# Gate table of the expert stage in stages of 64 tokens instead of 32, and the first gathered rows fetched after the last stage is stored

## The reference

```python
qry = (xb @ wq).reshape(blk, PEER_HEADS, 2, PEER_DHALF)
sc = jnp.einsum('thpd,hpkd->thpk', qry, subkeys)
s1, i1 = lax.top_k(sc[:, :, 0], 16); s2, i2 = lax.top_k(sc[:, :, 1], 16)
cand = (s1[..., :, None] + s2[..., None, :]).reshape(blk, 8, 256)
sf, ci = lax.top_k(cand, 16)
eid = e1 * 128 + e2                       # the two halves of the pick
g = softmax(sf)
act = gelu(einsum('td,thkd->thk', x, u_tab[eid]))
out = einsum('thk,thkd->td', g * act, v_tab[eid])
```

## Time and profile before

| | before |
|---|---|
| median of 3 runs | 4385.43 us (4378.03 to 4401.97) |
| profiled execution: its own time | 4393.77 us |
| profiled execution: span | 4392.1 us, granted TensorE clock 0.947 |
| TensorE (PE) busy | 3913.5 us, 89% |
| VectorE (DVE) busy | 2641.3 us, 60% |
| ScalarE (ACT) busy | 1313.7 us, 30% |
| GpSimd (POOL) busy | 1015.5 us, 23% |
| DMA, whole span | 985884 packets, 846.08 MB, 193 GB/s |

### The profile page before, as it was taken

One profiled execution on the slowest core, in us unless ns is written; L12 is line 12 of the kernel. 1 busy time (PEld: TensorE's weight loads), 2 busy tenths in 40 slices (PEclk: granted clock), 3 DMA queues, 4 the chain that ended last, 5 costly groups with the idle time before them and its releaser, 6 DMA issues.

```text
span 4392.1 us, 57633 instructions
## 1 busy us (share of the span) xinstructions
PE 3913.5 (89%) x21916; PEld 2057.0 (47%) x21916; DVE 2641.3 (60%) x4720; ACT 1313.7 (30%) x1836; POOL 1015.5 (23%) x672
## 2 busy tenths in 40 slices
PE   5999787799777899899999987999999999988987
PEld 3675342266533644455555543444444444444433
DVE  4232111577545405999899846667666766676765
ACT  4233111244224212333333332223323222222223
POOL 0000000223002000000000024444444455555642
PEclk8999898899789999999999998999999999999999
DMA  5232533422363215999977799888888899999993
GB/s 197 94 114 79 166 108 131 164 96 87 107 215 103 104 58 142 240 264 305 292 224 224 216 252 249 230 231 215 226 231 232 232 244 267 256 247 247 264 238 114
DMA packets 985884, 846.08 MB, mean 193 GB/s; under 512 B 755026, under 2 KB 835242, under 8 KB 978219
## 3 DMA queue, kind: packets, MB, share of 16 engines
q1 hardware_dynamic: 921540, 568.86, 51.9%
q0 software_dynamic: 60112, 215.78, 15.4%
q10 hardware_dynamic: 4032, 58.72, 3.3%
HBM read 620.46 MB, written 186.31 MB: 184 GB/s over the span
## 4 chain that ended last, share of the span: by engine, by line
DVE 20%; PE 14%; DMA 14%; SPq 4%; issue 4%; ACT 3%; POOL 2%; DVEq 0%; ACTq 0%; POOLq 0%
PE ex_psy L2940 9%; DMA ex_gate<-gate_all 8%; PE ex_psa L2908 4%; DMA ex_u<-in_peer_u_dram 4%; DVE rt_hotg L2659 2%; DVE rt_hote L2655 2%; SPq L2351 2%; DVE ex_acc L2783 2%; DVE ex_ulo L2615 2%; POOL ex_vlo L2458 2%; SPq L2411 2%; DVE ex_acc L2763 1%; DVE ex_wa L2797 1%; DMA ex_ug<-in_peer_u_dram,ex_idxp 1%; DVE rt_sc L2667 1%
## 5 line engine op out<-in xcount | busy, mean ns | idle before, releaser
L2940 PE MATMUL ex_psy<-ex_vhi,ex_wboth 128*128 128x512 f16 x3584 | 1107.7, 388 | 127.3 <-POOL ex_vlo L2458 77.9
L2908 PE MATMUL ex_psa<-h_hi,ex_uth 128*128 128x512 f16 (+1 forms) x2048 | 726.6, 355 | 32.1 <-DMA ex_utl<-ex_ulo 24.6
L2908 PE MATMUL ex_psa<-h_lo,ex_uth 128*128 128x512 f16 (+1 forms) x2048 | 726.5, 355 | 0.0
L2908 PE MATMUL ex_psa<-h_hi,ex_utl 128*128 128x512 f16 (+1 forms) x2048 | 726.3, 355 | 0.0
L2940 PE MATMUL ex_psy<-ex_vlo,ex_wboth 128*128 128x512 f16 x1792 | 694.4, 388 | 0.0
L2458 POOL TENSOR_TENSOR ex_vlo<-ex_v,ex_vhi 128x1024 f16<-128x1024 f32 x128 | 317.8, 2483 | 1420.2 <-ACT ex_vhi L2557 1419.9
L2940 PEld LDWEIGHTS ex_psy<-ex_vhi,ex_wboth 128*128 128x128 f16 x3584 | 356.9, 100 | 584.7 <-issue 141.1
L2548 ACT ACTIVATE ex_wboth<-ex_wa 128x896 f16<-128x896 f32 x128 | 121.6, 950 | 1080.4 <-DVE ex_wa L2797 1080.4
L2763 DVE TENSOR_TENSOR ex_acc<-ex_acc,ex_psy 128x512 f32<-128x512 f32 x434 | 289.3, 680 | 113.4 <-PE ex_psy L2940 113.2
L2908 PEld LDWEIGHTS ex_psa<-h_hi,ex_uth 128*128 128x128 f16 x2048 | 201.1, 98 | 217.7 <-DMA ex_utl<-ex_ulo 27.9
L2908 PEld LDWEIGHTS ex_psa<-h_hi,ex_utl 128*128 128x128 f16 x2048 | 201.2, 98 | 190.2 <-issue 5.2
(11 more groups left out here) (389 smaller groups left out, 6353.4 us busy)
## 6 DMA issues: line engine op xcount, KB each, us to landing
ex_u<-in_peer_u_dram SPq DMA_DIRECT2D x128, 512.0 KB, 5.8
ex_v<-in_peer_v_dram SPq DMA_DIRECT2D x128, 512.0 KB, 4.1
gate_all<-rt_stage ACTq DMA_DIRECT2D x28, 2048.0 KB, 7.1
ex_gate<-gate_all SPq DMA_DIRECT2D x128, 448.0 KB
act_all<-ex_wa SPq DMA_DIRECT2D x80, 448.0 KB, 3.3
ex_wa<-act_all SPq DMA_DIRECT2D x80, 448.0 KB, 4.8
ad_w<-in_ada_w_dram SPq DMA_DIRECT2D x8, 2048.0 KB, 9.9
sh_w<-in_w_in_dram SPq DMA_DIRECT2D x10, 1024.0 KB, 8.2
```

Source lines behind the costliest of these rows:

```text
L2908: mm = nc.tensor.matmul(ps_a[:, at:at + e - a], x[s][:, k, :], h[:, k, a:e], start=(k == 0 and j == 0), stop=(k == KD - 1 and j == 2))
L2940: mm = nc.tensor.matmul(sum_bank(q, n), w, v_[:, a * 512:(a + 1) * 512], start=(j == 0), stop=(j == len(mms) - 1))
```

## The change

`RUN` goes from 32 to 64. So `gate_all` has 14 stages of 64 tokens in place of 28 of 32, `stage` has two buffers of 32 KB a partition in place of 16 KB, a stage is full after 8 groups of 8 tokens and is stored as one DMA of 4 MB, and a block's gates are 14 runs of 256 bytes per partition. The larger buffers reach into the memory of `ug`, the buffers of the gathered u rows, so POOL's first three gathers (batch 0 of u), which were issued in the routing part, now wait until the last group is copied (`evac`) and both stage buffers are stored. SP's wait before the first v load (L2404) keeps its meaning: all stages stored. Memory moves: `wa` and `st` are allocated ahead of the routing buffers, and `same` takes the place of `cand`, which is dead when `same` is written.

```diff
-RUN = 32
+RUN = 64
...
+        wa = [sb(f"wa{s}", [P, DENSE]) for s in range(2)]
+        st = sb("st", [P, 6, PT + 1])
...
-            cand = ea("cand", [P, HEADS, TOPK * TOPK])
+            with nc.sbuf_tensor("rt_cand", [P, HEADS, TOPK * TOPK], F32) as cand:
+                pass
+            same = ea("same", [P, 2, HEADS, TOPK, TOPK], F16)
...
-            wa = [sb(f"wa{s}", [P, DENSE]) for s in range(2)]
-            st = sb("st", [P, 6, PT + 1])
...
                 pool.wait_ge(picked, 7)
                 pool.wait_ge(moved, 32)
+                pool.wait_ge(evac, GROUPS_A)
+                for e in range(2):
+                    pool.wait_ge(stage_stored[e], DENSE // RUN // 2 * 16)
                 gather("peer_u", ug, u_rows, 0, dotted)
...
-                    m, q = g // 4, g % 4
+                    m, q = g // (RUN // BT), g % (RUN // BT)
...
-                    if q == 3:
+                    if q == RUN // BT - 1:
```

More of the change, by code:

```diff
@@ L2271, in experts @@
             numbers = ea("numbers", [P, 2, HEADS, TOPK, TOPK], F16)
-            same = ea("same", [P, 2, HEADS, TOPK, TOPK], F16)
             ranks = ea("ranks", [P, TOPK, TOPK], F16)
```

## The result

| | before | after |
|---|---|---|
| median | 4382.27 us (4378.03 to 4401.97, 4 runs) | 4315.36 us (4307.24 to 4317.01, 4 runs) |
| ratio | | 0.9835, 95% interval 0.9802 to 0.9868 |
| profiled execution: span, clock | 4392.1 us, 0.947 | 4314.2 us, 0.954 |

The change makes the kernel 67 us faster.

The account below looks back on a forecast made before the run. From 1890 us on TensorE had the most work, with the gate load on nearly every group's path. Terms -27 - 29 - 6 + 32 + 5 = -25 us gave 4361 us from the median 4385.4; range 4322 to 4408.

Parts of the forecast that it names:

- Part 1, the gate load: Output part: half as many runs per gate load shorten VectorE's gate waits; -27, -29 and -6 us, together -62 us.
- 1.4 us a load: Output part: saving per gate load, somewhat under the 1.8 us bound from 3.4 us at 136 GB/s against 1.6 at 287.
- 62 of 100 us of idle time: Output part, after 2702 us: of TensorE's about 100 us idle, shorter gate loads and v's earlier issue recover 62.
- SP's relief makes TensorE the bound: Rival, output part: v and u leave SP's queue at once, the idle 100 us go; 4322 us, chance 0.15.
- Part 2, the stores: Routing part: 4 MB stores hold the next block's transposes 5.3 us longer, stalling TensorE; 22 plus 10, +32 us.
- what queues behind the transposes on SP: Routing part: the store of `wa`, for which ScalarE waits, and the next u load are delayed; +10 us.
- stores cost more than the reads gain: Rival, routing part transposes: 13 stores at 6 us cost 78 us against -62 and +5; 4406 us, chance 0.15.
- Part 3, the start: Start of the output part: longer last store 5.3, late u gathers 4.0, shorter gate loads -4; +5 us (0 to +10).
- The gates are not read faster: Rival, gate load: a 256-byte run takes as long as two of 128, nothing comes back; 4422 us, chance 0.10.
- mechanism of a wide pitch: Gate load: runs 4 MB apart instead of 2 might read slower; skill's copies: 103 GB/s against 164.
- The transposes are not held by the larger store: Rival, routing part: queues taken in turn let transposes between the store's packets, so stores cost nothing; 4328 us, chance 0.10.

Follow-up runs that it names:

- experiment 1: Changed kernel, but the table in DRAM stays in 28 stages of 32 tokens, so gates are read in 128-byte runs: 4435.33 us, ratio 1.0112 to the kernel before.
- experiment 2: Changed kernel with each block's gates read as two DMAs of 128-byte runs from the table of 64-token stages: 4443.8 us, ratio 1.0165 to the kernel before.
- experiment 3: Changed kernel with the first 7 stages of gates read in 256-byte runs, the last 7 as two DMAs of 128-byte runs: 4411.72 us, ratio 1.0072.
- experiment 4: Changed kernel with the gate load issued as three DMAs, all in 256-byte runs: 4353.26 us, ratio 0.9935 to the kernel before.
- Experiment 5: Kernel before with the gate loads issued from ScalarE's queue instead of SP's, still in 128-byte runs: 4353.12 us, ratio 0.9926.
- experiment 7: Changed kernel with each stage stored in four DMAs of 1 MB, one after every second group: 4269.25 us, ratio 0.9752 to the kernel before.
- experiment 8: Changed kernel with each stage stored as four DMAs of 1 MB, all issued together when it is full: 4307.45 us, ratio 0.9823 to the kernel before.
- experiment 9: Changed kernel with the store of `wa` issued ahead of the transposes on SP in the routing part: 4291.58 us, ratio 0.978 to the kernel before.
- Experiment 10: Kernel before with only POOL's new wait, holding the first three gathers of u rows: 4385.13 us, ratio 0.997.

## Why the prediction was off, by its own steps

**Part 1, the gate load: the step that failed.** The mechanism was right (experiments 1 to 4): fewer runs, shorter landing, less waiting at the group's end. The size was wrong in two terms.

- *1.4 us a load.* In the kept groups the landings in the chain shrank by 2.5 us (14.98 to 12.5), and VectorE's gate waits by 46 us where I had 27; in groups 21 on by 81 where I had 29. My price came from a window of 136 GB/s, read as a gate load running alone. That window lay at a load's tail. Among the fastest windows of 1 us in which gate packets alone moved, before and after:

```profile
2867.00:2868.00 1.00, 1.00 (x7) 0.42 (x5) 1.00 (x2) 0.39 (x1) 0.44 (x1) 1.00 1.38 212
```

```profile
3045.00:3046.00 1.00, 1.00 (x7) 0.46 (x5) 1.00 (x2) 0.97 (x2) 0.00 (x0) 1.00 1.28 277
```

At these rates 448 KB take 2.2 and 1.7 us, a saving of 0.5. So the price of a load alone would have been smaller still than mine, while the landing among others shrank by five times as much. The row to price it from was not the load alone but its landing, 15 us in a crowd. The 1.4 was close to something else, the DMA time that a load no longer takes: DMA share times length of the two stretches is 709 and 919 us before, 601 and 840 after, 1.5 us for each of 128 loads. That I took it for the shrinking of a wait was the error. That the other transfers took their share between each of its packets, so that half the packets waited half as often, fits; it was not shown by itself.

- *62 of 100 us of idle time, and nothing for the clock.* All but 13 us of the idle time went (-93). The clock gave 40 more. I had the rows for it, 37.91 against 36.42 us for the same 168 matmuls and 0.97, named the cost in the first paragraph, and left it out of the sum and of every rival.

The rival "SP's relief makes TensorE the bound" had the right end state, idle time gone, and with 0.15 too small a chance; its 4322 too lacked the clock. Its mechanism was a small part of it. In the kernel after v did not leave the queue at once: 51 issues took 179.2 us where they had taken 242.5. Experiment 5, which did free it, gives 32 to 65 us, with earlier gates in them. One issue of v took 2.40 us where the earlier trace rows had 9.07, another 15.13; that one stands in the chain, but TensorE was idle for only 0.05 us from 3900 to 3945:

```profile
3833.59 2.40 SPq L2412 DMA_DIRECT2D ex_v<-in_peer_v_dram  x1
...
3886.46 15.13 SPq L2412 DMA_DIRECT2D ex_v<-in_peer_v_dram  x1
```

**Part 2, the stores: right in place, +40 against +32.** The landing of 12.0 us (12.5 forecast) and the 10 waits for transposes (10 to 13 forecast) came as written; they were shorter (1.4 us each, not mostly 3). The mechanism held: the transposes stand back while a store runs (experiments 7 and 8). What I had as a remark, "what queues behind the transposes on SP", worth 10 us, was the larger half: 18 us of TensorE's waits in the window, 14 of them given back by one changed order (experiment 9). The rival "stores cost more than the reads gain" had the right path but the wrong balance.

**Part 3, the start: +5 against +15, of which most belongs to one execution's profile.** From the last one-hot product to the first unit the kernel before took 77.7 us and the one after 93.1, but the six kernels of experiments 1 to 4, 8 and 9, with the same stores and the same late gather, took 76.9 to 86.0, mean 80.2: +2.5. In the profile of after one gather of u rows in the chain there took 20.59 us to land; the longest such in experiments 8 and 9 took 8.64 and 8.87. Whether its other three executions had it too isn't known. Experiment 10 shows the late gather costing nothing that can be measured.

**The sum.** Forecast -62 + 32 + 5 = -25; measured -133 + 40 + 15 = -78 in the profile, -67 between the medians.

**The other rivals.** "The gates are not read faster" is out, and so is its mechanism of a wide pitch. The Trainium skill (DMA: Bandwidth & Descriptors, Latency and other measured facts) gives a lower rate for a row pitch of 4 MiB than of 2; here, with the pitch between the runs of one partition, the window with 4 MB between runs of 256 bytes moved 277 GB/s and the one with 2 MB between runs of 128 bytes 212, so no such loss shows. "The transposes are not held by the larger store" is out by experiments 7 and 8. The Trainium skill (the same page, Queues, rings and completion order) has the queues served in turn, packet by packet. The trace agrees: 31 packets of either queue in 2 us of the kernel after, 156 and 153 in 3 us of experiment 8. What I had wrong in that rival is what the rule gives here: it does let the transposes in between the store's packets, but 256 bytes for each 32 KB.

## What to carry to other kernels

Price a transfer on a loaded machine by its landing time among the others, not by its rate alone, and when a wait at a group's end goes, add what the lowered clock had cost: it was 30% of the gain here. Choose the run length of the read and the size of the write apart from each other: a stage can be laid out for wide runs and still be stored in small pieces, and the pieces should be shorter than the slack of whatever shares the DMA engines (here 1 MB was, 4 MB was not). Where one queue has small packets and another large ones at the same time, expect the small ones to stand. When a DMA is held in a queue, look at what is issued behind it before what waits for it.

## What the runs showed that I had not expected

- The number of DMAs has a price of its own: the gate load in three DMAs instead of one, same runs and bytes, made the output part 49 us longer, 0.38 us for each of 128 loads (0.30 by the medians).
- While 4 MB were being stored from ScalarE's queue, the second transpose took 7 to 8 us to leave SP's queue, and everything behind it stood; bursts of 1 MB left no such wait for TensorE.
- The store's queue and SP's are served packet for packet: 31 packets of 32 KB against 31 of 256 bytes in 2 us. Splitting the burst into DMAs with a quarter of the run length therefore changed nothing that shows; spacing them out gave back 49 us of routing part (2617.6 to 2569.1).
- On SP's queue a gate load left 7.1 us (median) after its buffer was free, because it stood behind v's load; on ScalarE's queue, 0.2 us.
